# Selecting the last two token tiles first, with 24 gathered dots in between

## The chip, the core and the metric

The kernel runs on one core of one Trainium2 chip. The metric is the device time of one launch in microseconds, from the first instruction to the last write. A core has TensorE (PE), VectorE (DVE), ScalarE (ACT), GpSimd (POOL), SyncE (SP, which only issues DMAs here) and 16 DMA engines.

## What is computed

One layer of a streaming encoder over 512 tokens of width 1024: a norm, a mixer (pooling and windowed attention), a norm, then a product-key retrieval over 16384 single-neuron experts, a gated embedding, and a last norm. What the change touches is the retrieval:

```python
q = (xt @ wq).reshape(T, PEER_HEADS, 2, PEER_HALF)
s = einsum('thpd,hpnd->thpn', q, subkeys)          # 8 heads, 2 sides, 128 keys
sv, si = top_k(s, 16)
comb = (sv[:, :, 0, :, None] + sv[:, :, 1, None, :]).reshape(T, PEER_HEADS, 256)
cs, ci = top_k(comb, 16)
idx = take(si[:, :, 0], ci // 16) * 128 + take(si[:, :, 1], ci % 16)
g = softmax(cs)
a = einsum('td,thkd->thk', x, u_tab[idx]);  w = g * gelu(a)
out = einsum('thk,thkd->td', w, v_tab[idx])
```

## The kernel before

Weights come as 298 tiles of 128 x 1024 f32 (512 KB). SP loads a tile into one of four slots of `raw`; ACT makes its high half (f16), DVE or POOL its low half, into `cut`; PE multiplies with both. A slot is free again when the low half four tiles back is made. The tiles are, in order: 10 + 8 of the mixer, 16 Q tiles (`T_Q` = 18 on), 8 G tiles (34 on), 128 U tiles (42 on), of which the last 40 alternate with V tiles, and then 88 V tiles (210 on).

**Q, G and the first 24 U tiles.** Each Q tile gives PE the scores of one head and side (`key_scores`), which ACT takes into `scores`. DVE meanwhile runs the selection: `top_k(head)` for eight heads, each over all four token tiles. A head is two passes: `top16` over the scores (maxima, their places, their replacement, line 1604 to 1615) and the sums of the two sides (`add_sides`, 1620 to 1628), then `top16` over the sums and `pick` (1635 to 1662). POOL makes the low halves of the 48 tiles from number 20 on (line 604), since DVE is taken. A table, `LOWS_IN_PASS`, says how many of them it may make from the start of which of the 16 passes on: DVE marks each start by `pass_begun` (1602). ACT makes the high half of tile n + 2 (`SPLIT_AHEAD`) around the output of tile n (`scale_and_split_hi`, 1027).

**Behind the selection** DVE makes the expert numbers (1682 to 1694), then biases, softmax, gates and the low halves of the next eight U tiles, the first of which stands two additions behind it (1701, 1388).

**Gates stage, 48 U tiles.** Dense gates are built for the first 352 tokens by one-hot products. The last tokens go another way: their experts' rows are gathered. POOL issues indirect DMAs (617), each of 128 rows of 4 KB, into eight slots (`expert_rows`, `ROW_RING`), and DVE forms a dot of a row with the token's hidden values (`dot`, 1754): first 32 for the last 32 tokens of token tile 2 (`EXTRA`, packed four heads' groups to the partitions), then 128 for tile 3, one per U tile here. Slot and count of `rows_in` are those of n modulo and by 8.

**Kept tiles, eights, late tiles.** Eight U tiles follow with 8 dots (`KEPT_DOTS`), then five eights of U and V tiles in turn (`both`) with `EIGHT_DOTS` = 24, 24, 24, 32 dots, and 26 sums (`EIGHT_SUMS`: a gathered V row times its weight, `add_row`, 1843), then eleven groups of eight late V tiles with the other 102 sums (`LATE_SUMS`). In these DVE also makes the weights (1812), their low halves (1836) and the tiles' low halves (1388); SP loads gates and, for late tiles, stored GELU outputs, four tiles at a time. The last eight tiles are ordered by token tile (`last_products`, 986), with the last norm behind them.

Of the kernel before, what the change touches and what calls it, by code (L numbers as in the profile page):

```python
# [27 lines left out]
F16 = mybir.dt.float16  # L28
# [34 lines left out]
SPLIT_AHEAD = 2  # L63
LOAD_AHEAD = 6
# [16 lines left out]
LOWS_IN_PASS = (5, 2, 3, 1, 3, 2, 3, 2, 3, 3, 4, 3, 5, 3, 5, 1)  # L81
assert len(LOWS_IN_PASS) == 16 and sum(LOWS_IN_PASS) == POOL_TILES
# [23 lines left out]
assert U_GATES - EXTRA + KEPT_DOTS + sum(EIGHT_DOTS) == HK and sum(EIGHT_SUMS) + sum(LATE_SUMS) == HK  # L106
assert len(EIGHT_DOTS) + len(EIGHT_SUMS) == EIGHTS and len(LATE_SUMS) + 1 == N_LATE // 8 and N_LATE % 8 == 0
assert EXTRA % ROW_RING == 0 and EXTRA % 8 == 0 and EXTRA < U_GATES - 8
# [22 lines left out]
def norm_batch(stage, i):  # L131

    return i // 2 if stage == 0 else 2 + TT * (stage - 1) + i

# [45 lines left out]
def layer(nc, tiles, u_rows, v_rows, x, ple_in, ple_w, norms, gate_b, small, pool_w, subkeys, alibi, ident, iota_oh, iota_k,  # L180
# [4 lines left out]
    with ExitStack() as ctx:  # L185
# [80 lines left out]
        top_v = part([2, TT, K])  # L266
        top_i = part([2, TT, K], U32)
# [4 lines left out]
        half_h = part([2, TT, K], F16)  # L272
# [277 lines left out]
        def _(pool):  # L550
# [46 lines left out]
            passes = [n for n, count in enumerate(LOWS_IN_PASS) for _ in range(count)]  # L597
            for i, n in enumerate(passes):
                t = Tile(POOL_FIRST + i)
                if n:  # L600
                    pool.wait_ge(pass_begun, n + 1)
# [5 lines left out]
            pool.wait_ge(ids_done, 1)  # L607
            for n, (table, ids, i) in enumerate([*((u_rows, extra_id, i) for i in range(EXTRA)),
                                                 *((u_rows, expert_id, i) for i in range(HK)),
                                                 *((v_rows, expert_id, i) for i in range(HK))]):  # L610
                if n == 4:
                    pool.wait_ge(ple_added, ND)
                    pool.wait_ge(gated, TT)
                if n == EXTRA:
                    pool.wait_ge(ids_done, 2)
                at_least(pool, rows_used, n - ROW_RING + 1)
                nc.gpsimd.indirect_dma_start(  # L617
                    expert_rows[n % ROW_RING], None, table,
                    bass.IndirectOffsetOnAxis(ap=ids[:, i:i + 1], axis=0)
                ).then_inc(rows_in[n % ROW_RING], 16)  # L620
# [392 lines left out]
        def _(act):  # L1013
# [194 lines left out]

            retrieve(0)
            with act.Fori(1, N_Q // 4) as it:  # L1210
                retrieve(it)
            for n in range(T_G, T_U):
                scale_and_split_hi(Tile(n + SPLIT_AHEAD))
# [21 lines left out]
            for j in range(4):  # L1235
                scale_and_split_hi(Tile(T_U + j + SPLIT_AHEAD))
                gelu(Tile(T_U + j), j, 0)
            with act.Fori(1, U_TOPK // 4) as it:
                for j in range(4):
                    t = Tile(T_U + j, 4, it)  # L1240
                    scale_and_split_hi(t.plus(SPLIT_AHEAD))
                    gelu(t, j, it)
            for j in range(U_SOFTMAX):
# [48 lines left out]
            with act.Fori(1, EXTRA // 8) as it:  # L1292
                build_gates(it)
            act.wait_ge(extra_turned, 1)
            nc.scalar.activation(extra_w, extra_w, ACT.Gelu).then_inc(extra_gelu, 1)
            for it in range(EXTRA // 8, U_GATES // 8 - 1):
# [85 lines left out]
        def _(dve):  # L1382
# [208 lines left out]
            def top16(number, values, index, source, spare):  # L1591

                rows_n = source.shape[1]
# [5 lines left out]

                settle()  # L1600
                at_least(dve, pass_begun, number)
                nc.vector.memset(pass_word[:], 0.0).then_inc(pass_begun, 1)
                for t in range(rows_n):
# [469 lines left out]
```

## Time and profile before

| | |
|---|---|
| median of 3 runs | 1340.71 us (1340.37 to 1341.3) |
| the profiled execution | 1342.04 us, its span 1339.9 us |
| mean granted TensorE clock | 0.992 |
| busy PE / PEld / DVE / ACT / POOL | 1289.0 / 713.7 / 1189.1 / 657.6 / 650.2 us |
| DMA moved | 401.87 MB, 300 GB/s over the span |
| largest DMA traffic | 402 to 1273 us: 350 to 400 GB/s |
| chain that ended last | DVE 34%, PE 32%, DMA 17%, issue 13% |

The stages by their times: mixer to 150 us, Q tiles to 247, G tiles to 289, the U tiles beside the selection to 382, gates to 626, kept tiles to 655, eights to 972, late tiles to 1305. "Busy" of PE is near 100% throughout, and its products are pipelined, so its busy share doesn't show small losses; these are found by counting products.

### The profile page before, as it was taken

To read this page: it belongs to the slowest core of one execution; us is meant where nothing else is said; L and a number is where in the kernel's file an instruction comes from. 1 tells how busy PE (TensorE), PEld (TensorE's weight loads), DVE (VectorE), ACT (ScalarE), POOL (GpSimd) and SP (SyncE) were. 2 spreads that over 40 slices of the span, in tenths; PEclk is the share of its full clock that TensorE was granted. 3 is DMA by queue.
4 is the path that set the end of the run, shared out by engine and by line. 5 is a ranking of instruction groups with operands and counts; after the bars stand their busy time and mean duration, and the time that the engine had idled before them with its cause. 6 is when DMAs were issued, how large, how long until landed. Compare 5 with 4: busy or idle time off the path is not lost.

```text
span 1339.9 us, 22847 instructions
## 1 busy us (share of the span) xinstructions
PE 1289.0 (96%) x7713; PEld 713.7 (53%) x7713; DVE 1189.1 (89%) x2390; ACT 657.6 (49%) x927; POOL 650.2 (49%) x379
## 2 busy tenths in 40 slices
PE   6999999999999999999999999989899999999987
PEld 3554555456666777777655555544344444444334
DVE  8866399999989999999699989979999998888997
ACT  5652555556676777776434343423333333333342
POOL 4741234436634433444266666756765455564602
PEclk9999999999999999999999999989899999999999
DMA  7231322336677999999999999999999999999972
GB/s 296 95 111 64 124 81 87 102 103 202 205 257 262 359 400 396 389 385 395 396 378 388 386 380 369 400 354 394 390 388 389 391 391 388 389 382 391 386 247 107
DMA packets 153603, 401.87 MB, mean 300 GB/s; under 512 B 12352, under 2 KB 72000, under 8 KB 151360
## 3 DMA queue, kind: packets, MB, share of 16 engines
q1 hardware_dynamic: 112064, 250.06, 52.4%
q0 software_dynamic: 41472, 151.01, 28.9%
q8 instruction: 30, 0.49, 0.2%
q14 instruction: 37, 0.30, 0.1%
HBM read 357.51 MB, written 42.99 MB: 299 GB/s over the span
## 4 chain that ended last, share of the span: by engine, by line
DVE 34%; PE 32%; DMA 17%; issue 13%; ACT 2%; SPq 1%; DVEq 0%; ACTq 0%
DMA area<-gelu_scratch 12%; PE bank L721 8%; PE bank L709 5%; PE bank L710 5%; PE bank L711 5%; DVE cut L1388 4%; DMA raw<-tiles_dram 4%; DVE cut L1395 3%; DVE ple_gate L1780 3%; DVE ple_gate L1843 3%; PE bank L986 2%; DVE area L1615 2%; DVE area L1656 2%; DVE area L1607 2%; DVE area L1609 2%
## 5 line engine op out<-in xcount | busy, mean ns | idle before, releaser
L721 PE MATMUL bank<-cut,area 128*128 128x512 f16 x2208 | 489.0, 381 | 14.9 <-DVE cut L1388 10.3
L709 PE MATMUL bank<-hT,cut 128*128 128x352 f16 (+1 forms) x1216 | 393.9, 324 | 9.8 <-DVE cut L1388 9.1
L711 PE MATMUL bank<-hT,cut 128*128 128x352 f16 (+1 forms) x1216 | 393.5, 324 | 0.0
L710 PE MATMUL bank<-hT,cut 128*128 128x352 f16 (+1 forms) x1216 | 393.5, 324 | 0.0
L1017 ACT ACTIVATE cut<-raw 128x1024 f16<-128x1024 f32 x246 | 257.2, 1054 | 239.2 <-DMA raw<-tiles_dram 224.8
L721 PEld LDWEIGHTS bank<-cut,area 128*128 128x128 f16 x2208 | 214.6, 98 | 278.3 <-DVE cut L1388 18.5
L1388 DVE SCALAR_TENSOR_TENSOR cut<-raw,cut 128x1024 f16<-128x1024 f32 x198 | 250.3, 1266 | 52.1 <-ACT cut L1017 51.6
L604 POOL TENSOR_TENSOR cut<-raw,cut 128x1024 f16<-128x1024 f32 x48 | 109.9, 2291 | 130.8 <-ACT cut L1027 114.5
L709 PEld LDWEIGHTS bank<-hT,cut 128*128 128x128 f16 x1216 | 119.2, 98 | 89.9 <-ACT gelu_out L1232 6.4
L711 PEld LDWEIGHTS bank<-hT,cut 128*128 128x128 f16 x1216 | 119.2, 98 | 75.7
L710 PEld LDWEIGHTS bank<-hT,cut 128*128 128x128 f16 x1216 | 119.2, 98 | 74.5 <-issue 0.3
L617 POOL DMA_INDIRECT ple_sb<-v_rows_dram,expert_id x64 | 111.8, 1746 | 75.5 <-DVE ple_gate L1843 69.1
L617 POOL DMA_INDIRECT ple_sb<-u_rows_dram,expert_id x64 | 101.7, 1590 | 92.2 <-DVE dots L1754 74.6
L1232 ACT ACTIVATE gelu_out<-bank 128x352 f32<-128x352 f32 x120 | 55.5, 462 | 176.1 <-PE bank L711 175.9
L1309 ACT ACTIVATE area<-area 128x384 f16<-128x384 f32 x128 | 66.0, 516 | 83.7 <-DVE area L1812 82.6
L1271 ACT ACTIVATE area<-bank 128x512 f32<-128x512 f32 x96 | 91.6, 1123 | 1.6 <-PE bank L930 1.4
L1843 DVE SCALAR_TENSOR_TENSOR ple_gate<-ple_sb,sparse_w,ple_gate 128x1024 f32<-128x1024 f32 x64 | 81.9, 1279 | 1.8
L1754 DVE CUSTOM_DVE_ANT_0 ple_sb<-ple_sb,hn 128x1024 f32<-128x1024 f32 x64 | 76.7, 1219 | 0.0
L1836 DVE TENSOR_TENSOR area<-area 128x384 f16<-128x384 f32 x128 | 70.5, 551 | 3.8 <-ACT area L1309 3.8
L617 POOL DMA_INDIRECT area<-v_rows_dram,expert_id x32 | 51.2, 1599 | 45.1 <-DVE ple_gate L1843 39.9
L617 POOL DMA_INDIRECT norm_rows<-v_rows_dram,expert_id x32 | 52.3, 1635 | 41.1 <-DVE ple_gate L1843 37.8
L617 POOL DMA_INDIRECT norm_rows<-u_rows_dram,expert_id x32 | 50.6, 1583 | 43.7 <-DVE dots L1754 33.8
(223 smaller groups left out, 1665.2 us busy)
## 6 DMA issues: line engine op xcount, KB each, us to landing
raw<-tiles_dram SPq DMA_DIRECT2D x298, 512.0 KB, 7.1
gates_scratch<-area SPq DMA_DIRECT2D x12, 2048.0 KB, 11.3
area<-gates_scratch SPq DMA_DIRECT2D x32, 768.0 KB, 10.4
gelu_scratch<-gelu_out SPq DMA_DIRECT2D x80, 192.0 KB, 5.5
area<-gelu_scratch SPq DMA_DIRECT2D x20, 768.0 KB, 12.7
norm_rows<-norms_dram SPq DMA_DIRECT2D x3, 1024.0 KB, 8.0
hn<-x_dram SPq DMA_DIRECT2D x4, 512.0 KB, 5.1
out_dram<-hn SPq DMA_DIRECT2D x3, 512.0 KB, 2.6
```

The lines of the kernel that those rows point to most:

```text
L604: nc.gpsimd.tensor_tensor(cut[:, t.slot, 1, :], raw[:, t.slot, :], cut[:, t.slot, 0, :], ALU.subtract).then_inc(lo_cut, 1)
L617: nc.gpsimd.indirect_dma_start(expert_rows[n % ROW_RING], None, table, bass.IndirectOffsetOnAxis(ap=ids[:, i:i + 1], axis=0)).then_inc(row ...
L709: nc.tensor.matmul(dst, w[0], hT[:, 0, k, 0:width], start=(k == 0), stop=False)
L710: nc.tensor.matmul(dst, w[0], hT[:, 1, k, 0:width], start=False, stop=False)
L711: last = nc.tensor.matmul(dst, w[1], hT[:, 0, k, 0:width], start=False, stop=(k == KD - 1))
L721: mm = nc.tensor.matmul(bank[:, 2 * tt + h, :], lhs(a)[:, tt * P:(tt + 1) * P], cut[:, t.slot, b, h * HALF:(h + 1) * HALF], start=(first a ...
L1017: nc.scalar.activation(halves_of(t)[:, 0, :], raw[:, t.slot, :], ACT.Copy, scale=t.scale).then_inc(hi_cut, 1)
L1271: nc.scalar.activation(gate_chunk[:, s, :, first:first + 4].rearrange("p n t -> p t n"), bank[:, four, :].rearrange("p (t n) -> p t n", t= ...
L1388: nc.vector.scalar_tensor_tensor(out=halves_of(t)[:, 1, :], in0=raw[:, t.slot, :], scalar=t.scale, in1=halves_of(t)[:, 0, :], op0=ALU.mult ...
L1754: nc.vector.tensor_tensor_reduce(slot, slot, values, 1.0, 0.0, ALU.mult, ALU.add, into).then_inc(rows_used, 1)
L1836: nc.vector.tensor_tensor(halves[:, 1, :], weight[:, slot, :], halves[:, 0, :], ALU.subtract).then_inc(weight_lo, 1)
L1843: nc.vector.scalar_tensor_tensor(out=sparse_sum, in0=expert_rows[n % ROW_RING], scalar=sparse_w[:, a:a + 1], in1=sparse_sum, op0=ALU.mult, ...
```

## The change

The selection is cut into nine units, each over some heads and some token tiles. `SELECTION` gives them: head 0 over all four token tiles; heads 1 and 2, 3 and 4, 5 and 6 over token tiles 2 and 3, head 7 over these (a half unit); then the same heads over tiles 0 and 1, the last a half unit again. Behind the fifth unit the numbers of all experts of token tiles 2 and 3 are known, and `number_rows` (moved from behind the selection) writes them. POOL then gathers 24 of the 32 `EXTRA` rows, four at a time through four slots, in turn with its low halves, and DVE dots them, four behind the score part and four behind the sum part of each of units 5, 6 and 7. `LOWS_IN_PASS` has 18 entries. ACT makes the high half of tile n + 3 in this stage (`SELECT_AHEAD`). The later stages start 24 dots further on: their counts of dots and sums change. Slot and turn of a row come from three small functions.

```diff
+SELECT_AHEAD = 3
-LOWS_IN_PASS = (5, 2, 3, 1, 3, 2, 3, 2, 3, 3, 4, 3, 5, 3, 5, 1)
+SELECTION = ((0, 1, 0, TT), (1, 2, 2, 2), (3, 2, 2, 2), (5, 2, 2, 2), (7, 1, 2, 2),
+             (1, 2, 0, 2), (3, 2, 0, 2), (5, 2, 0, 2), (7, 1, 0, 2))
+LATTER_HALF = 5
+LOWS_IN_PASS = (6, 1, 2, 1, 3, 1, 3, 1, 2, 1, 3, 6, 5, 6, 6, 1, 0, 0)
+DOTS_IN_UNIT = ((0, 0),) * 5 + ((4, 4), (4, 4), (4, 4), (0, 0))
-KEPT_DOTS = 8
-EIGHT_DOTS = (24, 24, 24, 32)
-EIGHT_SUMS = (26,)
-LATE_SUMS = (10, 10, 10, 10, 10, 10, 10, 10, 11, 11)
+EARLY_SLOTS = 4
+EARLY = sum(map(sum, DOTS_IN_UNIT))
+KEPT_DOTS = 12
+EIGHT_DOTS = (25, 25, 26)
+EIGHT_SUMS = (24, 20)
+LATE_SUMS = (9, 9, 9, 9, 8, 8, 8, 8, 8, 8)
...
+def row_slot(n):
+    return n % EARLY_SLOTS if n < EARLY else (n - EARLY) % ROW_RING
...
+            low, begun = POOL_FIRST, 0
+            for n, count in enumerate(LOWS_IN_PASS):
+                after = (n - 1) // 2 if n % 2 else n // 2 - 1
+                made = DOTS_IN_UNIT[after][0 if n % 2 else 1] if n else 0
+                gathers = EARLY_SLOTS if n == 2 * LATTER_HALF else made if begun + made <= EARLY else 0
+                gathers = min(gathers, EARLY - begun)
+                if n == 2 * LATTER_HALF:
+                    pool.wait_ge(ids_done, 1)
+                elif n:
+                    pool.wait_ge(pass_begun, n + 1)
+                for j in range(max(count, gathers)):
+                    if j < gathers:
+                        gather(begun)
+                        begun += 1
+                    if j < count:
+                        pool_low(Tile(low))
+                        low += 1
...
-                    scale_and_split_hi(t.plus(SPLIT_AHEAD))
+                    scale_and_split_hi(t.plus(SELECT_AHEAD))
...
+            def top_k(unit, first_head, heads, first_tile, tiles):
...
+                dve.wait_ge(scores_out, 2 * (first_head + heads))
+                begin_pass(2 * unit)
+                top16(rows_k(top_v_all), rows_k(top_i_all), [column(side, r) for side in range(2) for r in range(n)],
+                      replaced)
...
+                early_dots(DOTS_IN_UNIT[unit][0])
+                begin_pass(2 * unit + 1)
+                top16(sum_v, sum_i, [sums[:, r, :] for r in range(n)], sums_rep)
...
+                early_dots(DOTS_IN_UNIT[unit][1])
...
-            for head in range(HEADS):
-                top_k(head)
+            for unit, where in enumerate(SELECTION):
+                if unit == LATTER_HALF:
+                    number_rows()
+                    dve.wait_ge(extra_h_in, 16 * (P // TOK))
+                top_k(unit, *where)
...
-                        dot(8 * it + 4 * s + j)
+                        dot(EARLY + 8 * it + 4 * s + j)
...
-            first = U_GATES + KEPT_DOTS
+            first = EARLY + U_GATES + KEPT_DOTS
```

## Rows read from the trace of the kernel before

**Rows 1.** Chain that ended last, 640 to 700 us: start, length, what

```profile
665.80 3.89 PE bank L721 x18
673.26 3.89 PE bank L721 x18
```

**Rows 2.** Windows for L721: window, length, PE busy (x), PEld busy (x), PEclk, DMA, GB/s

```profile
882.00:975.90 93.90, 50.73 (x216) 21.40 (x217) 0.93 1.01 379
975.90:1295.00 319.10, 310.19 (x1424) 137.41 (x1422) 1.00 1.03 381
```

**Rows 3.** The same windows for L709 (L710 and L711 follow it)

```profile
882.00:975.90 93.90, 20.89 (x64) 6.47 (x64) 0.93 1.01 379
```

**Rows 4.** Timeline of PE where it paused: start, length, operation [idle before <-releaser]

```profile
384.56 0.32 PE L709 MATMUL bank<-hT,cut 128*128 128x352 f16 x1 [2.54 <-DVE cut L1388]
...
892.12 0.47 PE L709 MATMUL bank<-hT,cut 128*128 128x352 f16 x1 [5.95 <-DVE cut L1388]
...
1298.55 2.70 PE L986 MATMUL bank<-cut,area 128*128 128x512 f16 x6 [2.11 <-DVE cut L1388]
...
1305.02 2.33 PE L986 MATMUL bank<-cut,area 128*128 128x512 f16 x10 [1.67 <-DVE cut L1388]
```

**Rows 5.** Window behind the pause at 886: PE busy (x), granted clock, DMA

```profile
889.10:895.80 6.70, 3.68 (x13) 0.50 0.86 333
```

**Rows 6.** Waits, 975.9 to 1295 us: total, times, longest

```profile
DVE area L1812 <- issue: 24.8, 16, 3.4
```

**Rows 7.** Windows, kept tiles and late tiles: PE, PEld, DVE, ACT, POOL, clock, DMA

```profile
624.50:653.00 28.50, 28.50 (x213) 19.29 (x211) 18.12 (x31) 13.26 (x18) 8.98 (x8) 1.00 1.02 418
1039.00:1270.00 231.00, 222.84 (x1022) 98.33 (x1020) 206.10 (x242) 85.09 (x113) 122.86 (x72) 1.00 1.04 388
```

**Rows 8.** Timeline of DVE in the selection: marks of passes, one step twice, last step

```profile
166.94 0.06 DVE L1602 MEMSET pass_word<- 128x1 f32 x1
...
269.27 0.06 DVE L1602 MEMSET pass_word<- 128x1 f32 x1
...
282.36 0.06 DVE L1602 MEMSET pass_word<- 128x1 f32 x1
...
289.84 1.22 DVE L1653 TENSOR_TENSOR area<-area 128x2048 f16<-128x2048 f16 x1
...
295.19 0.06 DVE L1602 MEMSET pass_word<- 128x1 f32 x1
...
314.25 3.04 DVE L1653 TENSOR_TENSOR area<-area 128x2048 f16<-128x2048 f16 x1
...
323.13 0.06 DVE L1602 MEMSET pass_word<- 128x1 f32 x1
...
334.30 0.06 DVE L1602 MEMSET pass_word<- 128x1 f32 x1
...
378.21 0.19 DVE L1662 COPY area<-area 128x64 f32<-128x64 f32 x1
```

**Rows 9.** Timeline of POOL: three of its 48 low halves

```profile
156.75 2.12 POOL L604 TENSOR_TENSOR cut<-raw,cut 128x1024 f16<-128x1024 f32 x1 [3.00 <-ACT cut L1027]
162.82 2.12 POOL L604 TENSOR_TENSOR cut<-raw,cut 128x1024 f16<-128x1024 f32 x1 [3.95 <-ACT cut L1027]
...
313.09 3.12 POOL L604 TENSOR_TENSOR cut<-raw,cut 128x1024 f16<-128x1024 f32 x1 [1.28 <-ACT cut L1027]
```

**Rows 10.** Timeline of both engines in the mixer, 45 to 48 us

```profile
44.97 2.68 POOL L570 TENSOR_TENSOR hn<-hn,norm_rows 128x1024 f32<-128x1024 f32 x1
45.36 3.37 DVE L1388 SCALAR_TENSOR_TENSOR cut<-raw,cut 128x1024 f16<-128x1024 f32 x1
```

**Rows 11.** The dot's line: duration ns min/median/max, first and last start

```profile
L1754 DVE CUSTOM_DVE_ANT_0 ple_sb<-ple_sb,hn x64: 1216/1219/1222, 580.8 to 913.1; 128x1024 f32<-128x1024 f32 x64
```

**Rows 12.** The gathers' line: one group's durations, and landing of all

```profile
L617 POOL DMA_INDIRECT norm_rows<-u_rows_dram,area x8: 1212/1796/1941, 380.7 to 493.1; - x8
...
DMA to landing us min/median/max: 4.4/9.1/13.6
```

More of the change, by code:

```diff
@@ L596, in _, with pool_low @@
             pool.wait_ge(lo_cut, POOL_FIRST)
[L597 to L601, printed above, removed]
+            def pool_low(t):
                 pool.wait_ge(hi_cut, t.n + 1)
@@ L605, in _, with gather @@
                                         ALU.subtract).then_inc(lo_cut, 1)
[L607 to L611, printed above, removed]
+            def gather(n):
+                table = u_rows if n < EXTRA + HK else v_rows
+                ids = extra_id[:, n:n + 1] if n < EXTRA else expert_id[:, (n - EXTRA) % HK:(n - EXTRA) % HK + 1]
+                at_least(pool, rows_used, row_before(n) + 1)
+                nc.gpsimd.indirect_dma_start(
+                    expert_rows[row_slot(n)], None, table,
+                    bass.IndirectOffsetOnAxis(ap=ids, axis=0)
+                ).then_inc(rows_in[row_slot(n)], 16)
@@ L612, in _ @@
+            assert begun == EARLY and low == POOL_FIRST + POOL_TILES
+            pool.wait_ge(ids_done, 2)
+            for n in range(EARLY, EXTRA + 2 * HK):
+                if n == EARLY + EARLY_SLOTS:
                     pool.wait_ge(ple_added, ND)
                     pool.wait_ge(gated, TT)
[L614 to L620, printed above, removed]
+                gather(n)
@@ L1207, in retrieve @@
                 take_scores(4 * it + 3, 3)
+            for n in range(T_Q + SPLIT_AHEAD, T_Q + SELECT_AHEAD):
+                scale_and_split_hi(Tile(n))
             retrieve(0)
@@ L1291, in _ @@
             build_gates(0)
[L1292 to L1296, printed above, removed]
+            for it in range(1, U_GATES // 8 - 1):
+                if 8 * it == EXTRA - EARLY:
+                    act.wait_ge(extra_turned, 1)
+                    nc.scalar.activation(extra_w, extra_w, ACT.Gelu).then_inc(extra_gelu, 1)
                 build_gates(it)
@@ L1589, in _, with dot, early_dots, top16 @@
                 split_lo(Tile(n))
-            def top16(number, values, index, source, spare):
-                rows_n = source.shape[1]
+            def dot(n):
+                dve.wait_ge(rows_in[row_slot(n)], 16 * (row_turn(n) + 1))
+                own.settle()
+                own.mark(nc.vector.memset(word[:], 0.0))
+                slot = expert_rows[row_slot(n)]
+                values, into = (extra_h, extra_dots[:, n:n + 1]) if n < EXTRA else \
+                    (hn[:, ND, :], dots[:, n - EXTRA:n - EXTRA + 1])
+                nc.vector.tensor_tensor_reduce(slot, slot, values, 1.0, 0.0, ALU.mult, ALU.add,
+                                               into).then_inc(rows_used, 1)
+            dotted = [0]
+            def early_dots(count):
+                for _ in range(count):
+                    dot(dotted[0])
+                    dotted[0] += 1
+            def top16(values, index, source, spare):
                 def settle():
@@ L1618, in add_sides @@
                 own.settle()
[L1619 removed]
+                for r in range(n):
                     own.mark(nc.vector.tensor_tensor(
[L1621 to L1623 removed]
+                        sums[:, r, 0:WIDE * K].rearrange("p (a b) -> p a b", a=WIDE),
+                        top_v[:, 0, r, 0:WIDE].unsqueeze(2).to_broadcast([P, WIDE, K]),
+                        top_v[:, 1, r, :].unsqueeze(1).to_broadcast([P, WIDE, K]), ALU.add))
@@ new lines, in top_k @@
+                into = lambda w: picked[:, w, first_tile:first_tile + tiles,
+                                        K * first_head:K * (first_head + heads)].rearrange("p t (h k) -> p h t k", k=K)
+                each = lambda a: a.rearrange("p (h t) k -> p h t k", h=heads)
+                for side in range(2):
+                    r = slice(n * side, n * (side + 1))
+                    own.mark(nc.vector.tensor_tensor(into(side), each(hit[:, r, 0:K]), each(hit[:, r, K:2 * K]),
+                                                     ALU.add))
```

173 lines of the change are left out of this document (86 added, 87 removed).

## The prediction

> **What bounds the kernel now.** I read the busy tenths first, then PE's rate stage by stage, then what ended its pauses, then the passes of the selection on DVE. PE is the bound nearly everywhere: in the stage that alternates U and V tiles a pair takes 7.46 us, of which 3.89 are the 18 products of the V tile, 0.216 us each, so the 24 products of a U tile take 3.57, 0.149 each [rows 1]. Where it pauses can be counted. Between 882.0 and 975.9 us it makes 216 of the first kind and 64 x 3 of the second (the rows of the two sister lines count alike) [rows 2, 3]: 46.7 + 28.6 = 75.3 us of work in 93.9, so 18.6 are lost. Between 975.9 and 1295.0 it makes 1424 x 0.216 = 307.0 us of work in 319.1: 12.1 lost. Single pauses show who is late: 5.95 us before a low half, 2.11 and 1.67 in the last tiles, and 2.54 at 384.6, right behind the selection [rows 4]. A pause costs more than itself: after the one that ended at 892.12 the granted clock stayed at 0.50 (1.2 of 2.4 GHz) until 895.8 [rows 5], which makes some 2 us of the 18.6.
>
> Why the late stages lose: DVE waits there 24.8 us in 16 places for something no instruction releases, that is a landing [rows 6], and the core moves 388 GB/s at a DMA share of 1.04 for 231 us on end [rows 7]. Eight late tiles ask for 4.19 MB of tiles, 3.15 of gates and GELU outputs and ten rows of 0.52: 12.6 MB, at 388 GB/s 32.4 us, while PE needs 8 x 3.89 = 31.1. The difference, 1.3 in eight tiles, is the loss. The group with 32 dots is overloaded in the same way.
>
> The selection is the second stage that matters, and it is DVE's: it ends at 378.4, and 2.7 us of other work behind it stand the low halves for which PE waits until 384.56 [rows 4, 8]. PE has no slack against it, so what makes DVE's selection longer moves all that follows.
>
> **The change, part by part.**
>
> *Rows taken out of the full stages (a gain).* 24 dots move to the front, so eights 0 to 4 get 25, 25, 26 dots and 24, 20 sums for 24, 24, 24, 32 and 26, and the late groups 9 or 8 sums for 10 or 11. Nine rows make 12.1 MB, 31.1 us: equal to PE. Eight make 11.5, 29.7: under it. So of the 12.1 nearly all comes back, and the 18.6 too: 24 dots in an eight fitted before without a loss. In the last group DVE no longer arrives without a lead, and the pauses of 2.11 and 1.67 and their clock shrink: I take 4 us. Sum 34.7. Against it: the eight tiles before the first eight get 12 dots for 8 while that stretch already moves 418 GB/s [rows 7], and the third eight has 26. I leave 3 us lost for both (bounds 0 and 12). Gain 31.7, bounds 22 and 35.
>
> *Selection, first half (a gain).* A clear pass over the scores takes 334.30 - 323.13 = 11.2 us. A pass over the sums took 12.8 with one low of POOL in it. What a low costs: L1653 takes 1.22 clear and 3.04 where a low is in progress [rows 8, 9], so 1.9 with what follows, and a clear second pass 10.9. A clear head is 22.1, and eight are 176.6. They took 378.4 - 166.9 = 211.5: 35 us are lows of POOL, about 18 of the 48. The new table allows one low at the start of each second pass and few in the first ones, and the high halves one tile ahead let POOL make them there, in steps that it doesn't disturb. So the first four units run clear, but then wait for scores, which PE makes at a tile in 6.07 us (the distance of the lows in that stage) [rows 9]: the first pass begins with its scores at 166.9, and each of units 1 to 3 needs four tiles more, so they can't start before 191.2, 215.5 and 239.8. Unit 4 starts at 239.8 + 22.1 = 261.9, where the fifth head now starts at 269.27: 7.4 gained.
>
> *Selection, second half (the loss).* From 261.9: a half unit of 12.7 (its large steps halve, some 1.7 of small ones do not: estimate from a clear head), the row numbers 1.8 (moved here, so free behind the selection), three whole units 66.3, 24 dots at 1.22 [rows 11] 29.3, and the other half unit 12.7: 384.7 without any wait. Two things are added. Rows: the first gather at low traffic landed 4.4 us after its issue (the shortest of all; median 9.1) and takes POOL 1.2 at the least [rows 12]. Four gathers stand alternately with lows of 2.13, so the fourth is issued some 11 us into the pass and lands at 16 to 17, when the fourth dot wants it in a first pass of 11.2; a second pass with lows in it is late enough. I take 3 us (bounds 1 and 15). Lows: 27 of the 48 now fall into units 5 to 7, in passes of 3, 6, 5, 6, 6 and 1. A gather and a low take 3.4 us, so only two lows are done when the second pass reaches its two-input steps, 4.9 us in, and three when the first pass does, 9.9 in. By the same count 16 of the 27 fall on steps that POOL blocks, if the dots are such steps: 5, 2, 5 and 4 in passes 11 to 14. 16 x 1.9 = 31 us. Sum: 384.7 + 3 + 31 = 418.7. Less the 1.8 moved, against 378.4: the selection is late by 39 us.
>
> Does a low block a dot? No row shows one beside the other. The nearest is L1388, also f32 with two SBUF inputs of 1024: it took 3.37 instead of 1.22 where it began within a TENSOR_TENSOR of POOL [rows 10]. Beside gathers neither it nor the dot gets longer: the dot's longest of 64 is 1.222 [rows 11]. I take that a low blocks a dot. If not, about 9 of the 16 drop out, 17 us. The Trainium skill ("SBUF — State Buffer", Who interferes with whom) says that a DVE operation with both inputs in SBUF contends with GpSimd's reads, whichever began first blocking the other; the trace agrees for L1388, and by that rule the dearer sum holds. It speaks against this change.
>
> *PE behind it.* POOL's lows trail its gathers, so PE pauses some us here and there among the last 24 tiles of that stage, all hidden since it waits for DVE anyway; from 393 to about 423 it stands still. All 39 us arrive, and 2 more while the clock climbs back, as at 892 [rows 5]. Loss 41, bounds 22 (lows clear of dots, no row waited for) and 55.
>
> *At nothing:* the split into nine units beyond the price above, the slot arithmetic (done when the program is built), extra_h waited for earlier (its load stands before the Q tiles on SP's queue), the longer written-out ACT loop, and the gates stage, whose 48 dots stay 48.
>
> **Sum.** +41 - 31.7 = +9.3. The profiled execution took 1342.04 us with a span of 1339.9; the median of the runs is 1340.71, 1.3 below it. The difference is put on the median: 1350.
>
> **The rivals.** (A) The forecast: 1350, itself 1343 to 1358. (B) Faster: POOL's lows and the dots do not block each other, or POOL gets its lows done earlier in the pass than I count. Then the loss is 41 - 17 = 24 and the gain stands: 1333. For it: the first four units show that the table was laid out to keep lows off such steps; against it: [rows 10]. It wins as soon as fewer than 11 of the 27 lows fall on blocked steps. (C) Balance: half of the dots collide, or the units wait less: within 0.2%. (D) Slower still: rows come late. At the median landing of 9.1 us instead of 4.4 all six bursts wait, 3 to 5 us each, 15 to 20 more: 1364. The trace speaks against it, since DMA is a good deal less loaded there. The Trainium skill ("DMA: Bandwidth & Descriptors", SWDGE vs HWDGE vs iDMA) adds that descriptors made by GpSimd are held up while DVE has their shared port; a gather here takes 1.2 to 1.9 us [rows 12], so by the trace that is under 1 us each. (E) The refund fails: the denser tiles ahead of the first eight and its 26 dots push the raw loads late, and 10 us more stay lost: 1360. (F) It doesn't do what it says: PE isn't held by the selection's end. The pause at 384.56 with its releaser L1388 leaves this no room.
>
> **Chances.** A 0.44, B 0.28, C 0.12, D 0.08, E 0.07, F 0.01. Faster by over 0.2% (2.7 us, about what a measurement of this kernel can tell from no change): B and a part of A's lower edge, 0.30. Within: 0.13. Slower: 0.57. The range reaches into B and D: 1330 to 1365.
>
> **What would show it.** PE's pause before the first low half behind the selection: 25 to 32 us, from about 393 to 423 (B: 10 to 15). The pass marks: unit 4 near 262, unit 5 near 277, unit 8 near 405. In units 5 to 7 dots of 2 to 3.3 us beside lows of POOL; if they all take 1.22, B holds. L1653 and L1656 without lengthening in the first four units. Then the late stage: the same 1424 products in 308 to 309 us, DVE's waits for landings down from 24.8 to under 8, and no pause of over 2 us between 882 and 976 (shifted). The prediction is wrong if the selection's end moves by less than 25 us or the late stages keep more than 10 us of their loss.

## The result, and the profile after

The changed kernel takes 1351.49 us (median of six runs), beside 1342.94 for the kernel before on the same chip: a ratio of 1.0063, 95% interval 1.0039 to 1.0087. It is slower by 0.6%. The profiled execution took 1351.97 us with a span of 1350.0, 10.1 above the span of before. Forecast were +9.3 and 1350. The profiled execution of before was one of the quicker ones of its kernel (1342.04 us, where its medians beside the later runs are 1343.7 to 1344.9), so spans make the change look some 1 to 2 us dearer than medians do.

The page of the changed kernel: busy time of two engines, the busy tenths of PE, its clock, and two groups of instructions (busy us, mean ns, idle before it and the releaser).

```profile
PE 1286.9 (95%) x7713; PEld 716.5 (53%) x7713; DVE 1187.2 (88%) x2416; ACT 656.2 (49%) x927; POOL 612.1 (45%) x379
...
PE   6999999998865999999989999999999999999997
...
PEclk9999999999987999999999999999999999999999
...
L756 PE MATMUL bank<-hT,cut 128*128 128x352 f16 (+1 forms) x1216 | 395.8, 326 | 34.0 <-DVE cut L1442 25.4
...
L1894 DVE TENSOR_TENSOR area<-area 128x384 f32<-128x384 f32 x88 | 48.5, 551 | 32.0 <-issue 31.9
```

In slices 10 to 13 PE loses time and then stands still, and its clock falls. The timeline of PE has the two pauses (start, length, operation, idle before it), and a window has the clock behind the first:

```profile
419.01 0.48 PE L756 MATMUL bank<-hT,cut 128*128 128x352 f16 x1 [25.35 <-DVE cut L1442]
...
708.49 1.89 PE L768 MATMUL bank<-cut,area 128*128 128x512 f16 x4 [5.61 <-DVE area L1918]
...
419.00:426.00 7.00, 6.99 (x29) 0.60 0.77 237
```

PE resumes at 419.01 where it resumed at 384.56 before [rows 4]: 34.5 us later, and 2.7 more go while the clock is at 0.60, so the first tile behind the selection ends 37.2 us later. The second pause is new: tile 133, the first V tile of the first eight, ends 11.05 us after the tile before it, where such a tile takes 3.89 (7.2 lost with its clock).

The late stages, by windows over the same instructions as [rows 2, 3] (L768 and L756 are the lines that were L721 and L709); below them DVE's wait there (total, times, longest):

```profile
926.80:1001.95 75.15, 47.71 (x216) 21.09 (x216) 1.00 1.01 379
...
926.80:1001.95 75.15, 20.00 (x64) 6.26 (x64) 1.00 1.01 379
...
1001.95:1311.00 309.05, 307.65 (x1424) 138.81 (x1422) 1.00 1.00 370
...
DVE area L1894 <- issue: 31.9, 15, 4.2
```

The same 216 and 64 x 3 products take 75.15 us for 93.9: 18.7 back, all that was lost there. The same 1424 take 309.05 for 319.1: 10.0 back. From there to the span's end it is 39.0 us for 44.9: 5.9 back. The sum: 37.2 + 7.2 - 18.7 - 10.0 - 5.9 = 9.8 of the 10.1.

The selection itself. DVE's timeline, with the marks of its passes (L1692), steps of the picks (L1746, L1750), the widening copy (L1720) and early dots (L1653):

```profile
261.80 0.06 DVE L1692 MEMSET pass_word<- 128x1 f32 x1
...
275.98 0.06 DVE L1692 MEMSET pass_word<- 128x1 f32 x1
...
291.37 1.22 DVE L1653 CUSTOM_DVE_ANT_0 area<-area 128x1024 f32<-128x1024 f32 x1 [0.60 <-issue]
...
292.55 0.06 DVE L1692 MEMSET pass_word<- 128x1 f32 x1
...
304.25 3.04 DVE L1746 TENSOR_TENSOR area<-area 128x2048 f16<-128x2048 f16 x1
307.32 5.11 DVE L1750 TENSOR_TENSOR area<-area 128x1024 f16<-128x1024 f16 x3
...
314.29 1.22 DVE L1653 CUSTOM_DVE_ANT_0 norm_rows<-norm_rows,area 128x1024 f32<-128x1024 f32 x1
...
317.78 0.06 DVE L1692 MEMSET pass_word<- 128x1 f32 x1
...
328.51 4.78 DVE L1720 CAST area<-area 128x256 f16<-128x256 uint32 x1
...
338.14 0.06 DVE L1692 MEMSET pass_word<- 128x1 f32 x1
...
363.38 0.06 DVE L1692 MEMSET pass_word<- 128x1 f32 x1
...
374.11 6.87 DVE L1720 CAST area<-area 128x256 f16<-128x256 uint32 x1
...
385.83 0.06 DVE L1692 MEMSET pass_word<- 128x1 f32 x1
...
401.59 0.06 DVE L1692 MEMSET pass_word<- 128x1 f32 x1
...
407.51 0.06 DVE L1692 MEMSET pass_word<- 128x1 f32 x1
```

Unit 4 begins at 261.80 (forecast 261.9), unit 5 at 275.98, and the first half ran clear, as was said. The six passes of units 5 to 7 are 16.57, 25.23, 20.36, 25.24, 22.45 and 15.76 us long. The last has only one low half in it and four dots, so 15.8 is the clear length, and the lengthening is 0.8, 9.4, 4.6, 9.4, 6.6 and 0: 30.8 us. GpSimd's timeline shows beside what it falls:

```profile
302.70 0.96 POOL L638 DMA_INDIRECT area<-u_rows_dram,area  x1 [0.16 <-issue]
303.68 8.15 POOL L630 TENSOR_TENSOR cut<-raw,cut 128x1024 f16<-128x1024 f32 x3
...
327.93 0.96 POOL L638 DMA_INDIRECT area<-u_rows_dram,area  x1 [0.16 <-issue]
328.92 4.22 POOL L630 TENSOR_TENSOR cut<-raw,cut 128x1024 f16<-128x1024 f32 x2
```

In the second pass three low halves in a row lie on L1746 and L1750, and two before them hold up two small steps (L1729 and L1737, 1.91 and 2.68 us where some 0.2 is clear); in the first pass two lie on the copy. Then the low halves of the pass are done, and the dots, which stand last, find GpSimd idle: all 24 took 1.22 us. I had put some 9 of the 16 blocked steps on dots.

### The profile page after: what moved, and what is told of

It reads as the page before. It is cut to its first block, busy times and chain, and to the rows that moved or that the text cites. A ratio compares the mean times of both kernels' runs of the same rounds, so it can differ in the third digit from the quotient of the medians.

```text
span 1350.0 us, 22753 instructions
## 1 busy us (share of the span) xinstructions
PE 1286.9 (95%) x7713; PEld 716.5 (53%) x7713; DVE 1187.2 (88%) x2416; ACT 656.2 (49%) x927; POOL 612.1 (45%) x379
## 4 chain that ended last, share of the span: by engine, by line
PE 61%; DVE 19%; DMA 10%; issue 7%; ACT 2%; SPq 1%; DVEq 0%; ACTq 0%
PE bank L768 23%; PE bank L756 9%; PE bank L757 9%; PE bank L758 9%; DMA area<-gelu_scratch 3%; DMA raw<-tiles_dram 3%; DMA area<-gates_scratch 2%; PE bank L1033 2%; DVE cut L1442 2%; PE bank L783 2%; DVE ple_gate L1925 1%; DVE area L1686 1%; DVE area L1677 1%; DMA gates_scratch<-area 1%; DVE cut L1449 1%
## 5 line engine op out<-in xcount | busy, mean ns | idle before, releaser
L768 PE MATMUL bank<-cut,area 128*128 128x512 f16 x2208 | 485.0, 380 | 7.4 <-DVE area L1918 5.6
L756 PE MATMUL bank<-hT,cut 128*128 128x352 f16 (+1 forms) x1216 | 395.8, 326 | 34.0 <-DVE cut L1442 25.4
L768 PEld LDWEIGHTS bank<-cut,area 128*128 128x128 f16 x2208 | 215.9, 98 | 265.4 <-DVE area L1918 6.2
L756 PEld LDWEIGHTS bank<-hT,cut 128*128 128x128 f16 x1216 | 119.6, 98 | 114.7 <-DVE cut L1442 25.7
L630 POOL TENSOR_TENSOR cut<-raw,cut 128x1024 f16<-128x1024 f32 x48 | 105.4, 2208 | 90.5 <-DVE pass_word L1692 57.3
L638 POOL DMA_INDIRECT ple_sb<-v_rows_dram,expert_id x64 | 97.4, 1522 | 107.0 <-DVE ple_gate L1925 100.9
L638 POOL DMA_INDIRECT area<-v_rows_dram,expert_id x32 | 47.3, 1479 | 65.3 <-DVE ple_gate L1925 62.7
L1894 DVE TENSOR_TENSOR area<-area 128x384 f32<-128x384 f32 x88 | 48.5, 551 | 32.0 <-issue 31.9
L1653 DVE CUSTOM_DVE_ANT_0 ple_sb<-ple_sb,hn 128x1024 f32<-128x1024 f32 x64 | 76.5, 1218 | 0.0
```

The source lines that it names most:

```text
L638: nc.gpsimd.indirect_dma_start(expert_rows[row_slot(n)], None, table, bass.IndirectOffsetOnAxis(ap=ids, axis=0)).then_inc(rows_in[row_slot ...
L756: nc.tensor.matmul(dst, w[0], hT[:, 0, k, 0:width], start=(k == 0), stop=False)
L768: mm = nc.tensor.matmul(bank[:, 2 * tt + h, :], lhs(a)[:, tt * P:(tt + 1) * P], cut[:, t.slot, b, h * HALF:(h + 1) * HALF], start=(first a ...
L1653: nc.vector.tensor_tensor_reduce(slot, slot, values, 1.0, 0.0, ALU.mult, ALU.add, into).then_inc(rows_used, 1)
```

## The experiments

Ratios are to the kernel before, run beside the others on the same chip (median 1344.92 us for e1 to e4, 1343.73 for e5, e6, e8 and e9, 1343.88 for e10 to e12). Where a kernel's lines are shifted the rows say so themselves.

**e1: the new order without the early rows.** Nine units, the new table of low halves, high halves three ahead; all 32 extra rows dotted in the gates stage and the counts per group as before.

```diff
-DOTS_IN_UNIT = ((0, 0),) * 5 + ((4, 4), (4, 4), (4, 4), (0, 0))
+DOTS_IN_UNIT = ((0, 0),) * 9
-KEPT_DOTS = 12
-EIGHT_DOTS = (25, 25, 26)
-EIGHT_SUMS = (24, 20)
-LATE_SUMS = (9, 9, 9, 9, 8, 8, 8, 8, 8, 8)
+KEPT_DOTS = 8
+EIGHT_DOTS = (24, 24, 24, 32)
+EIGHT_SUMS = (26,)
+LATE_SUMS = (10, 10, 10, 10, 10, 10, 10, 10, 11, 11)
...
-                gathers = EARLY_SLOTS if n == 2 * LATTER_HALF else made if begun + made <= EARLY else 0
+                gathers = made
```

> Nine units in the new order, the new table of low halves and the high halves one tile further ahead, but no early dots: all 32 + 128 dots stand where they stood before, with the counts of before. Account (dots and the lows beside them make the selection late, not the order): units start as in the changed kernel up to 276 us, then 66 us for units 5 to 7, 10 to 12 of the 27 lows lengthen a step by 1.9 each, and the selection ends near 375, before PE gets there at 381; the pause before the first low half behind it (2.5 us before the change) is gone; late stages lose their 30 us as before. 1338 us, 1335 to 1342. Rival (cutting it into nine units is what costs): the selection ends after 395 and the time is 1350.

Measured: 1340.29 us, ratio 0.9964 (0.9952 to 0.9975). The new order, with its table and the high halves further ahead, is worth 0.4% by itself. The marks (count, durations, first and last start), and PE between 290 and 380 us:

```profile
L1692 DVE MEMSET pass_word<- x18: 59/59/59, 167.0 to 369.6; 128x1 f32 x18
...
290.00:380.00 90.00, 90.00 (x605) 1.00 0.61 205
```

The last mark stands at 369.6 for 407.5 in the changed kernel, PE never stops, and it doesn't pause behind the selection: that ends at 376.6, the first low half is there 4 to 5 us behind it as in the changed kernel (414.4 and 419.01), and PE wants it at 381.9. So the selection is just in time, with under 1 us of slack. Beside the kernel before, the pause of 2.54 us is gone and the first V tile starts 2.7 us sooner (662.97 for 665.63), but the spans differ by 1.1 us and the medians by 4.6: what makes up the rest wasn't traced. The 24 rows cost it 37.9 us: their dots stand 1.15 us apart (27.6), and 10.3 us are low halves, which without gathers between them fall on fewer steps that they block (passes 9, 11, 13 and 15 are lengthened by some 20 us in all here).

**e2: the early rows left out.** The changed kernel with its 24 early rows neither gathered nor dotted (their dots are set to zero). Its time is that of the refund without its price.

```diff
-    return (n - EARLY) // ROW_RING + (EARLY // EARLY_SLOTS if row_slot(n) < EARLY_SLOTS else 0)
+    return (n - EARLY) // ROW_RING
...
                     if j < gathers:
-                        gather(begun)
                         begun += 1
...
-                    dot(dotted[0])
+                    own.settle()
+                    nc.vector.memset(extra_dots[:, dotted[0]:dotted[0] + 1], 0.0).then_inc(rows_used, 1)
```

> The changed kernel with the 24 early rows left out altogether: neither gathered nor dotted, their dots are set to zero (part of the last 32 tokens of tile 2 is then not computed). All later counts are those of the changed kernel. Account: selection as in the kernel with the order alone, and the whole refund of the late stages, 28 to 31 us: 1309 us, 1305 to 1314. The difference to the order alone is the refund, the difference to the changed kernel (1351) is what the 24 dots cost in the selection, some 38 to 42 us. Rival (the late stages got faster for another reason than 24 rows less, or the refund isn't 30): 1320 to 1340.

Measured: 1313.16 us, ratio 0.976 (0.974 to 0.9779), span 1313.0. Against e1's 1338.8 the refund is 25.8 us, and against the changed kernel's 1350.0 the price is 37.0. Those two numbers are the case: the rows cost 1.54 us each where they went and gave 1.08 us each where they came from. These are spans of single executions. The medians give 27.1 for the refund and 38.3 for the price (the latter against 1351.49, which was measured beside other runs), or 1.13 and 1.60 us a row.

**e3: kept tiles at 8 dots.** The new pause at the first eight stands where DVE waits for gates:

```diff
-KEPT_DOTS = 12
-EIGHT_DOTS = (25, 25, 26)
+KEPT_DOTS = 8
+EIGHT_DOTS = (26, 27, 27)
```

```profile
706.72 1.03 DVE L1894 TENSOR_TENSOR area<-gelu_out,area 128x384 f32<-128x384 f32 x2 [7.29 <-DMA area<-gates_scratch]
```

> The changed kernel with 8 dots instead of 12 in the eight kept tiles, and 26, 27, 27 instead of 25, 25, 26 in the first three eights. Account: DVE's wait of 7.3 us for the first gates load at 706 us comes of the fuller kept tiles (gates are stored and loaded beside 12 row gathers) and goes; PE's pause of 5.8 us there and its slow clock behind go with it, -7 us; the three fuller eights may give 1 to 4 back: 1346 us, 1343 to 1349. Rival (the pause comes of the shifted phase, not of the rows): the pause stays and the time is 1351 to 1353.

Measured: 1350.32 us, ratio 1.0044 (1.0026 to 1.0063). Half a miss. That wait is gone, and tile 133 takes 3.89 us again, but PE pauses later instead; this is the longest of its pauses there:

```profile
906.92 0.47 PE L756 MATMUL bank<-hT,cut 128*128 128x352 f16 x1 [2.35 <-DVE cut L1442]
```

Tile 210, behind the eights with dots, ends at 1002.13 us for 1001.95 in the changed kernel. PE reaches tile 133 5.2 us sooner and is no sooner at tile 210: moving four dots within this stretch moves the loss. That the stretch is full of bytes (385 to 396 GB/s in e3) is my reading of why; no run varied the bytes alone. The term is real, but it can't be saved by this split. Every run here with 12 kept dots waited 5.6 to 7.3 us at that place, and none with 8 more than 0.4.

**e4: high halves two tiles ahead, as before.**

```diff
-SELECT_AHEAD = 3
+SELECT_AHEAD = 2
```

> The changed kernel with high halves two tiles ahead in the selection, as before the change. Account (POOL can make a low at the start of a pass only if its high is there): while PE works on Q tiles each low comes up to 6 us later, the single lows of passes 3, 5, 7 fall on two-input steps of DVE (+1.9 each) and L1750 takes 2.5 where it takes 0.7; unit 4 starts up to 3 us later (the wait for scores hides the rest); with U tiles lows come one tile later too, 2 to 5 more of them collide. 1355 us, 1352 to 1362. Rival (it makes no difference, since the ring of four tiles and not the order on ACT sets the high halves): 1351.

Measured: 1351.76 us, ratio 1.0039 (1.0013 to 1.0065), whose interval holds the 1.0063 of the changed kernel. I had expected 1355 and the rival's time held: in this kernel the third tile ahead is worth nothing that can be measured. PE's pause behind the selection is 25.91 us for 25.35. The run shows one thing more. Low halves come later in it, and four of the 24 dots have one beside them:

```profile
333.26 3.14 DVE L1653 CUSTOM_DVE_ANT_0 area<-area 128x1024 f32<-128x1024 f32 x1
336.34 3.13 DVE L1653 CUSTOM_DVE_ANT_0 area<-area 128x1024 f32<-128x1024 f32 x1
```

Yet its six passes sum to 125.0 us, for 125.6 in the changed kernel, where no dot is held up. The low halves moved from the picks and the copy to the dots, and the price stayed.

**e5: the gathers first.** In each pass all four gathers, then the low halves.

```diff
-                for j in range(max(count, gathers)):
-                    if j < gathers:
-                        gather(begun)
-                        begun += 1
-                    if j < count:
-                        pool_low(Tile(low))
-                        low += 1
+                for j in range(gathers):
+                    gather(begun)
+                    begun += 1
+                for j in range(count):
+                    pool_low(Tile(low))
+                    low += 1
```

> Only GpSimd's order in a pass changes: the four gathers stand ahead of all the low halves of the pass, so that low halves fall beside the widening copy and the early dots, which in the changed kernel had none beside them (all 24 took 1.22 us). If a low half holds up a dot as it does the steps of the picks (the account of the prediction), dots of 2.3 to 3.3 us appear in the passes with five or six low halves, the lengthening of the passes stays at 31 us give or take 5, and the time at 1351 us (1347 to 1356). If a dot isn't held up, every dot stays at 1.22 us, some three low halves of each unit run beside the dots for nothing, which takes about 3 x 3 x 1.9 = 17 us from the selection, and the time is about 1335 us.

Measured: 1360.22 us, ratio 1.0111 (1.0089 to 1.0133). Slower than either theory said, and for the first one's reason. The early dots of the second pair of slots (durations min/median/max), and one of them beside a low half of GpSimd:

```profile
L1652 DVE CUSTOM_DVE_ANT_0 area<-area x12: 1214/1219/3139, 290.4 to 408.7; 128x1024 f32<-128x1024 f32 x12
...
337.27 3.14 DVE L1652 CUSTOM_DVE_ANT_0 area<-area 128x1024 f32<-128x1024 f32 x1
...
337.06 2.26 POOL L630 TENSOR_TENSOR cut<-raw,cut 128x1024 f16<-128x1024 f32 x1 [3.28 <-ACT cut L1073]
```

A low half does block a dot, by 1.9 us, so the step of the prediction that no row of before could show is right, though the changed kernel never paid it. My error was the size: with the gathers in front more low halves end up beside steps that they block, not as many. The six passes lengthen by 39 us for 31 (16.97, 27.70, 21.14, 27.60, 23.07, 17.73), and the last mark goes from 407.5 to 415.9.

**e6: the low halves spread.** All 24 rows; the table flattened, and in a second pass two low halves ahead of the gathers.

```diff
-LOWS_IN_PASS = (6, 1, 2, 1, 3, 1, 3, 1, 2, 1, 3, 6, 5, 6, 6, 1, 0, 0)
+LOWS_IN_PASS = (6, 1, 2, 1, 3, 1, 3, 1, 2, 1, 3, 4, 4, 4, 4, 4, 2, 2)
...
+                order = "LL" + "G" * gathers if n % 2 else "GLGLGLG"[:7] if gathers else ""
...
```

> All 24 early dots stay; the low halves of the second half of the selection are put 4, 4, 4, 4, 4, 2, 2 over the passes instead of 6, 5, 6, 6, 1, 0, 0, in the second pass of a unit two of them ahead of the gathers, so that more of them run while VectorE searches (one input, not held up in the trace). If the 31 us by which the passes are lengthened come from low halves beside two-input steps, about half goes: the selection ends some 15 us earlier, the pause behind it falls from 25.5 us to about 10, and the time is 1336 us (1332 to 1342). If the number of gathers and dots and not the place of the low halves sets the passes, the marks stay where they are and the time stays at 1350 us.

Measured: 1339.36 us, ratio 0.9971 (0.9959 to 0.9984): 12 us under the changed kernel with the same work. The last mark and PE's waits between 290 and 412 us:

```profile
L1703 DVE MEMSET pass_word<- x18: 59/59/59, 166.8 to 395.8; 128x1 f32 x18
...
PE bank L767 <- POOL cut L630: 18.4, 8, 4.2
```

The lengthening is down to 19 us and the last mark comes 11.7 us earlier, with 24 gathers and 24 dots as before, so it is the place of the low halves that sets it. PE waits for late low halves of GpSimd 18.4 us in eight small pieces and then 2.0 us behind the selection, where the changed kernel has 7.5 us in three pieces and one standstill of 25.4, and its clock stays at 1.00 between 380 and 426 us, where it was 0.70.

**e10: a table between the two** (3, 5, 5, 5, 4, 4, 1, 0 over the last eight passes; the diff is to e6).

```diff
-LOWS_IN_PASS = (6, 1, 2, 1, 3, 1, 3, 1, 2, 1, 3, 4, 4, 4, 4, 4, 2, 2)
+LOWS_IN_PASS = (6, 1, 2, 1, 3, 1, 3, 1, 2, 1, 3, 5, 5, 5, 4, 4, 1, 0)
```

> 24 early rows, order within a pass as in e6, low halves 3, 5, 5, 5, 4, 4, 1, 0 over the eight passes: between the table of the changed kernel and the one of e6. In e6 the passes were lengthened by 19.1 us, and TensorE, which lost 25.5 us behind the selection in the changed kernel, lost 21.7 us between 290 and 380 us waiting for low halves that came late, and started its 69th tile only some 10 us after the selection. Here the low halves come early enough for 20 us passes; each one more in the first five passes costs up to 1.9 us of VectorE. The account gives a lengthening of 23 us, the 69th tile at 408 us instead of 412, and 1335 us (1331 to 1341). Rival: TensorE's last low half and the selection end together whatever the table, since GpSimd has 24 gathers and 27 low halves to make in either: 1339 us as in e6.

Measured: 1345.0 us, ratio 1.0013 (1.0001 to 1.0025). A miss on both sides: worse than e6.

```profile
L1703 DVE MEMSET pass_word<- x18: 59/59/59, 166.3 to 401.2; 128x1 f32 x18
...
412.57 0.48 PE L767 MATMUL bank<-hT,cut 128*128 128x352 f16 x1 [11.24 <-DVE cut L1453]
```

I had counted PE's small waits in e6 as a loss that could be won back. They were free: PE then came just in time for DVE. With earlier low halves PE arrives 5.4 us sooner, DVE ends 5.4 us later, and the difference is a standstill of 11.24 us with a slow clock behind it.

**e12: the low halves cut short.** The changed kernel, but the 27 low halves of the second half cover 32 of their 1024 columns; the rest of them isn't computed.

```diff
+                w = slice(0, D if t.n < POOL_FIRST + sum(LOWS_IN_PASS[:2 * LATTER_HALF]) else 32)
-                nc.gpsimd.tensor_tensor(cut[:, t.slot, 1, :], raw[:, t.slot, :], cut[:, t.slot, 0, :],
+                nc.gpsimd.tensor_tensor(cut[:, t.slot, 1, w], raw[:, t.slot, w], cut[:, t.slot, 0, w],
```

> The changed kernel with GpSimd's low halves of the second half of the selection (27 of them) cut to 32 of their 1024 columns: the rest of these low halves isn't computed. Order, gathers, dots and waits stay. By the account all of the 30.8 us by which passes 10 to 15 are lengthened is the price of those low halves beside two-input steps: the marks then follow at 11.1 us, and at 15.8 us where four dots stand in the pass, the selection ends near 383 us, the 69th tile ends at 388 to 392 us instead of 425, and the time is 1316 us (1312 to 1322). If the gathers (24 there too, with their descriptors) or the landing rows lengthen the passes, a part stays: with half of it 1331 us, with all of it 1351 us.

Measured: 1333.06 us, ratio 0.9925 (0.9903 to 0.9946). Expected were 1316, or 1331 if half of the lengthening were due to something else. Read by the total alone this would say "half". The timeline of DVE and the waits (total, times, longest) say otherwise:

```profile
299.14 1.23 DVE L1747 TENSOR_TENSOR area<-area 128x2048 f16<-128x2048 f16 x1
300.40 1.48 DVE L1751 TENSOR_TENSOR area<-area 128x1024 f16<-128x1024 f16 x3
...
343.88 1.22 DVE L1654 CUSTOM_DVE_ANT_0 area<-area 128x1024 f32<-128x1024 f32 x1 [3.47 <-issue]
...
POOL cut L631 <- ACT cut L1075: 46.7, 21, 3.3
```

The steps are all clear (1.48 us where 5.11 stood), so the low halves were the whole of the 31 us. But GpSimd is now faster than PE and ScalarE can give it tiles: it waits 46.7 us for high halves, and the gathers stand behind those waits in its queue. So rows come late, and DVE waits 12.2 us before six dots: 107.1 us for the six passes, of which 94.9 are the clear length. This is rival D's wait, by another cause than the landing time.

**e8, e9 and e11: fewer early rows.** Order within a pass as in e6. e8 has 8 early rows and e6's table; e9 has 16; e11 is e8 with another table. The rows given back go to the stages behind. The lines that set the order within a pass are those of e6 and are left out of the diff.

```diff
-DOTS_IN_UNIT = ((0, 0),) * 5 + ((4, 4), (4, 4), (4, 4), (0, 0))
+DOTS_IN_UNIT = ((0, 0),) * 5 + ((4, 4), (0, 0), (0, 0), (0, 0))
-LOWS_IN_PASS = (6, 1, 2, 1, 3, 1, 3, 1, 2, 1, 3, 6, 5, 6, 6, 1, 0, 0)
+LOWS_IN_PASS = (6, 1, 2, 1, 3, 1, 3, 1, 2, 1, 3, 5, 4, 4, 3, 4, 2, 2)
-KEPT_DOTS = 12
-EIGHT_DOTS = (25, 25, 26)
-EIGHT_SUMS = (24, 20)
-LATE_SUMS = (9, 9, 9, 9, 8, 8, 8, 8, 8, 8)
+KEPT_DOTS = 8
+EIGHT_DOTS = (24, 24, 24, 24)
+EIGHT_SUMS = (28,)
+LATE_SUMS = (10, 10, 10, 10, 10, 10, 10, 10, 10, 10)
```

(The diff is e11's.)

> Order and low halves as in e6, but 8 early rows instead of 24; the 16 others go back to the kept tiles, the first eights and the late eights (kept 8, eights 24 24 24 24 and 28, late 10 each). From the runs with none and with 24 rows: the refund was 25.8 us for 24, so 8.6 us for 8 if it is even; the selection of the new order alone ended some 6 us ahead of TensorE, and 8 dots cost 9 to 12 us there, of which 3 to 6 are left to pay, less what the spreading gives back. 1338.8 - 8.6 + 3 = 1333 us (1328 to 1338). Rival: the refund comes only with the last rows taken away (it is set by one eight that is over the limit): then about 1339 us.

> As e8 with 16 early rows (kept 8, eights 22 22 22 22 and 30, late 10 10 10 10 10 10 10 10 9 9). Refund 17.2 us if even; the dots cost 18 us plus 4 to 8 of low halves in the selection, less 6 of slack and less what the spreading gives back (0 to 10): 1338.8 - 17.2 + 16 = 1338 us without the latter, 1331 with it; 1333 us, 1327 to 1341. Rival (the price per row rises with their number, since each row's dot moves low halves beside the picks): e9 is slower than e8 by 5 us or more.

> e8 (8 early rows) with the low halves 3, 5, 4, 4, 3, 4, 2, 2 instead of 3, 4, 4, 4, 4, 4, 2, 2. In e8 TensorE lost 4.6 us between 290 and 380 us at low halves that came late, all of it in the two passes with dots (302 and 311 us); behind the selection it lost nothing. One low half more in the first of these passes takes up to 3.6 us of that away and puts at most 1.9 us on VectorE, which ends ahead of TensorE. 1331 us (1329 to 1335); rival: 1334.6 us as e8, if the low half is late because of GpSimd's own queue in that pass (four gathers and three waits) and not because of the table.

Measured: e8 1334.64 us, ratio 0.9931 (0.9913 to 0.995); e9 1342.19, ratio 0.9987 (0.9974 to 0.9999); e11 1332.83, ratio 0.9915 (0.9898 to 0.9931). e8 and e11 lie in their ranges. e9 is a miss: it lies above its range of 1327 to 1341, by its rival, 7.6 us slower than e8. e11 doesn't tell its expectation from its rival: its interval and e8's overlap, and their spans are alike, so the other table is not shown to gain anything. PE in the late tiles of e11 and of e9 (busy, count, clock, DMA), and e11's marks:

```profile
L1703 DVE MEMSET pass_word<- x18: 59/59/59, 166.4 to 370.9; 128x1 f32 x18
...
980.00:1270.00 290.00, 281.86 (x1288) 0.99 1.04 387
...
980.00:1270.00 290.00, 283.18 (x1296) 0.99 1.04 386
```

With 8 early rows the last mark stands at 370.9 for e1's 369.6: eight dots, 9.2 us, are nearly covered by low halves that no longer block (not by slack, as my expectation had it; there is none in e1). The spans of e8 and e11, 1330.5 and 1330.8 us, are 8 us under e1's.

The start of the first V tile parts price from refund. Up to it e8 is 4.7 us behind e1 (667.66 for 662.97), e11 3.0 and e9 14.4; of that PE lost 15 us between 290 and 380 in e9, to low halves that come late for it (505 products for e1's 605). From it to the end of the span e1 takes 675.8 us, e8 662.8, e11 664.9 and e9 662.5: 13.0, 10.9 and 13.3 back. So 8 rows bring back some 40 to 50% of what 24 rows do (25.8), some 10 of it up to the last U tile, a stretch in which no eight has 32 dots any more, and the next 8 bring nothing. With ten rows in a late eight PE works 281.86 of 290 us, with 9.8 still 283.18, with 9 or 8, in the changed kernel, it is 288.60. So the refund has steps and the price rises row by row: 8 rows are the cheap ones. e11 beats both kernels, by 0.85% the one before and by 1.5% the changed one.

## Why the prediction was right, point by point

**The sign and size.** +41 - 31.7 was forecast, +37.2 + 7.2 - 34.6 was measured. Both sides were off by some 4 us, the loss 3.8 too high and the net gain 4.3 too high, and that these cancel to 0.8 us is luck; each term by itself was right to within 5 us.

**Selection, first half.** Right to 0.1 us (unit 4 at 261.80), with the wait for scores as worked out. The steps of the picks (L1746, L1750) have their clear length there, as the sign asked. e1 shows in addition that without the rows this order is a gain.

**Selection, second half.** Lengthening forecast 16 x 1.9 = 31 us, measured 30.8. By pass the forecast was 5, 2, 5 and 4 blocked steps in passes 11 to 14 and the trace has 9.4, 4.6, 9.4 and 6.6 us, or 5, 2.4, 5 and 3.5 steps of 1.9. e12 shows that it is all due to low halves, since with these cut short each step is clear. The sizes that were off: dots stand 1.15 us apart, not 1.22 (1.7 us less), and rows were waited for 0.60 us, not 3. Unit 8 began at 401.59 for about 405. The last mark came at 407.5, and the steps behind it brought the end to 414.4 for 418.7.

**Does a low block a dot.** The rule taken was right (e4 and e5, 3.14 us for 1.22), but the place was wrong. The sign named for rival B, dots that all take 1.22, was met, and B didn't come: the low halves had spent their price on the picks and on the copy before the dots began. The sign tested the place of the collision, not its price; the length of the passes would have been the right one.

**PE behind it.** The pause, 25.4 us from 393 to 419, lies in the forecast's 25 to 32, and the clock cost 2.7 for 2. So 37.2 for 41 follows from the end of the selection alone.

**Rows taken out of the full stages.** 18.6 and 10.0 came back where 18.6 and nearly all of 12.1 were said, the tail gave 5.9 for 4. The mis-sized term is what was left for the denser kept tiles and the 26 dots: 3 us forecast, 7.2 measured in one place. e3 shows that a lighter load there moves the loss behind it, by the same amount. Bounds of 0 and 12 had held it.

**DVE's waits for landings** were to fall from 24.8 to under 8 us. They rose to 31.9, and PE lost almost nothing beside them. That sign was badly chosen. PE works 307.65 of 309.05 us there, so DVE waits for gates that PE doesn't need yet; my reading, which no run tests, is that with fewer rows DVE is simply done sooner. Such a wait measures DVE's lead, and only PE's own pauses measure a loss.

**The rivals.** B's and E's mechanisms both exist (e6 and e12 for what fewer collisions bring, the pause at the first eight for E). D's wait was 0.60 us in the changed kernel; it grows to 12.2 when GpSimd outruns PE (e12), by another cause than D named. C, within 0.2%, lies outside the interval of 1.0039 to 1.0087. F is excluded by e1 and e2: what the selection's end gains or loses reaches the end of the kernel nearly whole.

**What stays open.** Why the gates land 7 us late at the first eight with 12 kept dots wasn't taken apart: which of SP's transfers stand ahead of them was not tried. That it goes with the 12 is shown by all runs with 12 and with 8. Nor was the split of e11 between eights and late tiles tuned, where PE is idle for 8.1 of 290 us.

## What to carry to other kernels

Work moved from a full stage to a stage with a chain of its own is paid there by its duration plus what it displaces: here each row's dot cost 1.15 us, and gathers in GpSimd's queue pushed low halves onto steps that they block, which made 1.54 of it, against 1.08 us of refund (1.60 and 1.13 by the medians). Before moving all, try a part: 8 of the 24 rows brought over 40% of the refund and moved the last mark of the selection by 1.3 us and the first V tile by 3.0 (e11). And when the order of a second engine's queue decides what it collides with, judge a table by when the bounding engine arrives, since small waits before a point where it must wait anyway are free, and shorter than a standstill that also costs clock.

## What the runs showed of the hardware

A DVE operation can be passed over more than once. The widening copy, 0.3 us when clear (0.28 in e5), took 4.78 us beside two low halves of GpSimd back to back and 6.87 beside three: GpSimd went from one to the next at its full speed (4.22 us for two) and DVE got no turn between. It had begun 0.41 us ahead of them, while GpSimd was at the end of a gather (327.93 to 328.89), and at 374.11 the same. Larger steps on DVE do alternate: L1746 and the three of L1750 took 8.1 us where 2.7 are clear, while three low halves took 8.15 for 6.4. Before, I knew one collision as 1.9 us whichever step it hit, which holds for the sum but not for a short step. The Trainium skill ("SBUF — State Buffer", Who interferes with whom) names casts among the operations that can take the port pair they share with GpSimd, and the trace agrees; it also says that whichever began first has the pair for its whole instruction. Copies in two other runs tell what that means for the gather. In e2, without gathers, a copy began 0.02 us ahead of a low half, took its clear 0.28 us, and the low half took 2.26 for 2.13:

```profile
316.15 0.28 DVE L1720 CAST area<-area 128x256 f16<-128x256 uint32 x1
...
316.17 2.26 POOL L630 TENSOR_TENSOR cut<-raw,cut 128x1024 f16<-128x1024 f32 x1 [1.45 <-ACT cut L1073]
```

In e4 one began in the last 0.4 us of a gather (329.69 to 330.65) with no low half behind it, and ended 0.1 us after the gather (0.47 us). So the trace agrees with that rule too, if the end of a gather counts for GpSimd: the copy came second to it, and a low half followed 0.03 us behind the gather and went ahead of the copy again. What in a gather does this isn't shown; a two-input step earlier in one took its clear 0.34 us (L1716 at 328.25).

Indirect gathers were cheaper than the rows of before let expect: 0.93 to 0.97 us on GpSimd between low halves in the selection of the changed kernel (the first 1.21), 1.80 in the median of [rows 12]; in e12 four that ran beside a step of the picks or a dot took 1.77 to 1.95. The dots took no harm from them: the longest in e12 is 1.25 us.
